# Gate and up products of 25 experts in each MoE layer as 512-column products on two column groups

## What is computed

```python
def hier_moe(h, rg_w, rg_b, re_w, re_b, w_gate, w_up, w_down):
    # top-1 of 4 groups, then top-2 of its 8 experts: 32 experts, 512 (token, expert) pairs
    ...
    def expert_block(args):
        xr, e = args
        return (jax.nn.silu(xr @ w_gate[e]) * (xr @ w_up[e])) @ w_down[e]
    ...
    out = jnp.zeros((T, D), jnp.float32).at[row_tok].add(y * row_w[:, None])
```

## Time and profile before

| | us |
|---|---|
| median of 3 runs (2040.75 to 2042.89) | 2042.81 |
| the profiled execution's own time | 2039.13 |
| its span, first to last instruction | 2037.3 |
| PE busy in the span | 1929.5 (95%) |
| DVE busy | 879.4 (43%) |
| ACT busy | 672.0 (33%) |
| first MoE layer, from its gather to its last combine | about 46 to 492 |
| second MoE layer | about 598 to 1036 |

### The profile page before, as it was taken

How to read it: one execution, slowest core, us unless ns; L and a number is a source line. 1 busy time by engine, 2 the same in 40 slices (tenths; PEclk the granted TensorE clock), 3 DMA queues, 4 the chain that set the end, 5 groups by cost and what they waited for, 6 DMA issues and landing times. The chain is left out here.

```text
span 2037.3 us, 36364 instructions
## 1 busy us (share of the span) xinstructions
PE 1929.5 (95%) x16096; PEld 1379.6 (68%) x16096; DVE 879.4 (43%) x1396; ACT 672.0 (33%) x1138; POOL 61.3 (3%) x99
## 2 busy tenths in 40 slices
PE   7999989888999999999989999999999999999998
PEld 6544444445984444434468888878888888987887
DVE  4111111104740111111165656875655665786663
ACT  2000000004530000000054546674545564675552
POOL 0000000000000000000020000010000000011000
PEclk8999999999999999999999999999999999999999
DMA  9999999998679999999975545335545555425551
GB/s 406 431 430 431 430 431 430 432 428 348 266 294 434 428 429 431 432 431 429 425 287 200 189 163 206 124 134 216 188 165 207 199 189 183 166 99 186 191 194 65
DMA packets 48992, 598.33 MB, mean 294 GB/s; under 512 B 5428, under 2 KB 5940, under 8 KB 8884
## 3 DMA queue, kind: packets, MB, share of 16 engines
q1 hardware_dynamic: 47664, 592.43, 71.9%
q10 hardware_dynamic: 1156, 3.42, 0.5%
HBM read 594.78 MB, written 1.05 MB: 292 GB/s over the span
## 5 line engine op out<-in xcount | busy, mean ns | idle before, releaser
L2006 DVE TENSOR_TENSOR SPLIT<-RING,SPLIT 128x2048 fp32r<-128x2048 f32 (+2 forms) x178 | 398.9, 2256 | 139.4 <-ACT SPLIT L1484 139.3
L1484 ACT ACTIVATE SPLIT<-RING 128x2048 fp32r<-128x2048 f32 (+2 forms) x178 | 332.7, 1887 | 42.0 <-DMA RING<-in_units 42.0
L1149 PE MATMUL PS<-HTB,SPLIT 128*128 128x512 f32 x1152 | 289.1, 393 | 0.0
L747 PE MATMUL PS<-RING,WK 128*32 128x128 f32 x8192 | 259.7, 274 | 18.0 <-issue 13.7
L781 PE MATMUL PS<-WK 128*32 128x512 f32 x560 | 250.6, 601 | 23.2 <-DVE WK L2275 20.6
L747 PEld LDWEIGHTS PS<-RING,WK 128*32 128x32 f32 x8192 | 229.7, 109 | 51.3 <-issue 48.6
L1632 ACT ACTIVATE WK<-PS 128x128 f32<-128x128 f32 x64 | 17.8, 278 | 688.0 <-PE PS L747 688.0
L1149 PEld LDWEIGHTS PS<-HTB,SPLIT 128*128 128x128 f32 x1152 | 207.4, 189 | 37.3
L781 PEld LDWEIGHTS PS<-WK 128*32 128x32 f32 x560 | 59.3, 111 | 189.3 <-issue 162.1
L2268 DVE TENSOR_TENSOR WK<-WK,PS 128x128 f32<-128x128 f32 x64 | 18.4, 288 | 341.7 <-ACT WK L1632 341.7
L1152 PEld LDWEIGHTS PS<-HTB,SPLIT 128*128 128x128 f32 x1152 | 157.2, 190 | 11.3
(11 more groups left out here) (342 smaller groups left out, 2295.1 us busy)
## 6 DMA issues: line engine op xcount, KB each, us to landing
RING<-in_w_gu SPq DMA_DIRECT2D x54, 4096.0 KB, 33.3
RING<-in_units SPq DMA_DIRECT2D x171, 1024.0 KB, 4.8
WK<-in_w_down SPq DMA_DIRECT2D x37, 2048.0 KB, 31.3
RING<-in_w_gu SPq DMA_DIRECT2D x20, 2048.0 KB, 13.6
RING<-in_w_down SPq DMA_DIRECT2D x18, 2048.0 KB, 32.1
SEAT<-in_w_down SPq DMA_DIRECT2D x7, 2048.0 KB, 34.6
RING<-in_units SPq DMA_DIRECT2D x4, 768.0 KB, 12.0
RB<-in_rows ACTq DMA_DIRECT2D x6, 512.0 KB, 3.8
```

Of the source, the lines that this page charges most:

```text
L747: t = pe.matmul(PS[32 * q:32 * q + 32, pb, z * 128:z * 128 + 128], mo.XE[:, g % 2, c, 32 * i:32 * i + 32], v[:, c, 128 * q:128 * q + 128], ...
L1149: pe.matmul(out.rearrange("p (z b n) -> p z b n", z=2, b=2), hi(c), HTB[:, :, :, c, :], start=c == 0, stop=False)
L1484: ac.activation(unit_part(u, 0), loaded(u), ACT.Copy).then_inc(s_hi, 1)
L2006: dv.tensor_tensor(unit_part(u, 1), loaded(u), unit_part(u, 0).bitcast(F32), ALU.subtract).then_inc(s_lo, 1)
```

## The change

`slim(e)` holds for experts 5 to 29 of both layers. For these:

- `gate_up` runs 16 products of 512 columns: chunk c of gate on column group 0 (outputs on partitions 0 to 31), chunk c of up on column group 1 (partitions 32 to 63), in turns. Both semaphores are raised on the last pair.
- silu reads 32 x 512 from partitions 0 to 31 of the bank and writes partitions 32 to 63 of HW (the same memory as HG); the product with up is 32 x 512 and goes to partitions 64 to 95 or 96 to 127 of HW, by the expert's parity.
- `turn_hidden` is four transposes of 32 x 128 into 128 x 32 each, one per quarter of the hidden width.
- silu waits, besides what it waited for, until the product of the expert before has been made (s_hg); where the layout changes (experts 5 and 30) until the expert before has been turned (s_ht).

The down products, the gather, the combine, the loads, and experts 0 to 4, 30 and 31 are as they were. The diff, cut to its core:

```diff
+def slim(e):
+    return 5 <= e < 30
...
             def gate_up(e):
...
+                if slim(e):
+                    pe.wait_ge(*landed(("both", l, e)))
+                    v = slab(("both", l, e))[:, 0:2 * SLOT].rearrange("p (z c n) -> p z c n", z=2, c=8)
+                    for c in range(8):
+                        if i == 0 and c % 4 == 0:
+                            pe.wait_ge(s_xe, evicted(l, g, c // 4))
+                        for z in range(2):
+                            t = pe.matmul(PS[32 * z:32 * z + 32, pb, :], mo.XE[:, g % 2, c, 32 * i:32 * i + 32],
+                                          v[:, z, c, :], start=c == 0, stop=c == 7)
+                            if c == 7:
+                                t.then_inc(s_up if z else s_gate, 1)
+                    return
...
-                pe.transpose(PS[:, 3, 0:128], mo.HG[:, 2 + e % 2, :], ident).then_inc(s_ht, 1)
+                if slim(e):
+                    rows = slice(64 + 32 * (e % 2), 96 + 32 * (e % 2))
+                    for f in range(4):
+                        t = pe.transpose(PS[:, 3, 32 * f:32 * f + 32], mo.HW[rows, 128 * f:128 * f + 128], ident[rows, rows])
+                    t.then_inc(s_ht, 1)
...
-                        ac.activation(mo.HG[:, pb, :], PS[:, pb, 0:128], ACT.Silu).then_inc(s_silu, 1)
+                        if slim(e):
+                            ac.wait_ge(*((s_hg, 32 * l + e) if slim(e - 1) else (s_ht, 32 * l + e)))
+                            ac.activation(mo.HW[32:64, :], PS[0:32, pb, :], ACT.Silu).then_inc(s_silu, 1)
+                        else:
+                            if slim(e - 1):
+                                ac.wait_ge(s_ht, 32 * l + e)
+                            ac.activation(mo.HG[:, pb, :], PS[:, pb, 0:128], ACT.Silu).then_inc(s_silu, 1)
...
-                        dv.tensor_tensor(mo.HG[:, 2 + pb, :], mo.HG[:, pb, :], PS[:, pb, 128:256],
-                                         ALU.mult).then_inc(s_hg, 1)
+                        if slim(e):
+                            dv.tensor_tensor(mo.HW[64 + 32 * pb:96 + 32 * pb, :], mo.HW[32:64, :], PS[32:64, pb, :],
+                                             ALU.mult).then_inc(s_hg, 1)
```

More of the change, by code:

```diff
@@ L342, in build @@
         mo.GT = al(512).rearrange("p (k n) -> p k n", k=2)
-        mo.HG = al(512).rearrange("p (k n) -> p k n", k=4)
+        mo.HW = al(512)
+        mo.HG = mo.HW.rearrange("p (k n) -> p k n", k=4)
         mo.HE = al(256).rearrange("p (k n) -> p k n", k=2)
@@ L763, in turn_hidden @@
                     pe.wait_ge(s_he, 32 * l + e)
-                pe.transpose(PS[:, 3, 0:128], mo.HG[:, 2 + e % 2, :], ident).then_inc(s_ht, 1)
+                if slim(e):
[4 more added lines that the diff above has]
+                else:
+                    pe.transpose(PS[:, 3, 0:128], mo.HG[:, 2 + e % 2, :], ident).then_inc(s_ht, 1)
             def down(e):
@@ L2267, in step @@
                         dv.wait_ge(s_silu, 32 * l + e + 1)
-                        dv.tensor_tensor(mo.HG[:, 2 + pb, :], mo.HG[:, pb, :], PS[:, pb, 128:256],
-                                         ALU.mult).then_inc(s_hg, 1)
+                        if slim(e):
+                            dv.tensor_tensor(mo.HW[64 + 32 * pb:96 + 32 * pb, :], mo.HW[32:64, :], PS[32:64, pb, :],
+                                             ALU.mult).then_inc(s_hg, 1)
+                        else:
+                            dv.tensor_tensor(mo.HG[:, 2 + pb, :], mo.HG[:, pb, :], PS[:, pb, 128:256],
+                                             ALU.mult).then_inc(s_hg, 1)
                     if e:
```

## The result

The change made the kernel slower, by about the amount forecast. The medians are 2192.06 us (2190.41 to 2193.38, 4 runs) after it and 2042.18 us (2040.75 to 2042.89, 4 runs) before it, a ratio of 1.0735 with a 95% interval of 1.0723 to 1.0748. The forecast was 2196, in a range of 2180 to 2225. The profiled executions stand at 2193.38 and 2039.13 us, 154.3 apart; the sum was made against that one and came to +153.

The account below looks back on a forecast made before the run. Transfers (58.9 us per group) and PE (54.6) stood close, with PE the bound after. 92.0 us per layer, 184 for both, less 22.8 and 8, gave +153: 2042.8 to 2196 us, range 2180 to 2225.

Parts of the forecast that it names:

- The bound: MoE layers: transfers at 58.9 us per group of four stand close above PE's 54.6; changed, PE bounds at 69.3.
- cover: MoE layers: PE has 4.3 us per group, about 1.1 us per expert, before a longer step makes it the bound.
- Part 1: Gate_up products: two column groups run side by side, 7.0 us instead of 3.63, +3.37 us per expert.
- Rival 4: Gate_up: the column groups take turns at 512 columns, +343 us, about 2540; 4%.
- Part 2: Steps with i = 1: gate_up starts before down ends, gaining 1.67 us each, 11.7 us per layer.
- Part 3: From gate_up's end to down: longer silu and product add 0.72 us, 0.80 for i = 0; 19.4 us per layer.
- Part 4: MoE layers: weight waits (8.2 us) and "issue" stalls (14.6) vanish, together 22.8 us, plus 8 us from half clock.
- Rival 3: The 12 spots with i = 0, between gate_up and down: clock falls anew, +20 up to 40 us, 2216 to 2236; 10%.
- Rival 2: PE's "issue" stalls in gate_up stay, so 14.6 us and 8 us of half clock come back, 2219; 9%.
- rival 5: MoE layers: not slower, the transfers stay the bound and cover it all, 2020 us; 3%.

Follow-up runs that it names:

- e4_one_in_four: Kernel before with the change for only one expert in four (5, 9, ... 29; seven a layer): 2076.93 us, ratio 1.018.
- e5_gate_then_up: Changed kernel with all eight gate products on column group 0 first, then all eight of up on group 1: 2430.43 us, single run.
- e3_clear_of_down: Changed kernel with gate and up of i = 3 (six experts a layer) on column groups 2 and 3 instead of 0 and 1: 2174.67 us.
- e1_copy_first: Changed kernel with DVE's copy of the turned hidden values put ahead of the product with up in each step: 2150.13 us, ratio 1.0527.
- e6_light_loads: Kernel before, gate and up loads for experts 8 to 29 cut to 6144 of 8192 columns (output not the reference's): 2024.51 us.
- e10_light_copy_first: Kernel before with gate and up loads of experts 8 to 29 cut to 6144 of 8192 columns, and DVE's copy ahead of the product: 2011.37 us.

## Why the prediction was right

**The bound** (PE takes over from the transfers). Right: no wait for weights is left, and a group takes 69.2 us, 69.3 forecast. What the prediction says of cover, that up to 4.3 us per group would be free, was wrong (e4_one_in_four), but its sum subtracts PE's waits and makes no use of it.

**Part 1, gate_up.** Right: 6.99 us for a forecast of 7.0. Down of experts 30 and 31 had been the proper row for whether column groups run side by side at more than 128 columns. Rival 4 falls by this number, and e5_gate_then_up shows the condition it stands on: the products for the two groups in turns.

**Part 2, the start ahead of down.** Right: from the start of down to the turn 12.17 us (170.46 to 182.63), 12.18 by the sum, and the experiments of either sign. The Trainium skill, page "TensorE: Matmul & The Clock Gate", section "The mechanism", has matmuls in strict program order; for products on different column groups no trace here agrees, from 157.44 against 158.72 to 273.71 against 274.13 in e3_clear_of_down.

**Part 3, the tail.** The mechanism was right (e1_copy_first), two sizes were off and nearly cancelled. All engines in the i = 1 step, which answers to the earlier trace rows:

```profile
182.63 0.43 PE L785 MATMUL PS<-CS,WK 32*128 32x32 f32 x4
182.77 0.59 ACT L1658 ACTIVATE WK<-PS 32x512 f32<-32x512 f32 x1 [4.62 <-PE PS L746]
183.39 0.68 DVE L2299 TENSOR_TENSOR WK<-WK,PS 32x512 f32<-32x512 f32 x1 [4.10 <-ACT WK L1658]
184.11 0.29 DVE L2309 COPY WK<-PS 128x128 f32<-128x128 f32 x1
```

silu took 0.59 and the product 0.68, as the rows of 128 partitions had it. But the copy used to start 0.09 us before the product ended, and now it starts just behind it, so the tail grew by 0.79 to 0.86 us instead of 0.72: +4 us in all. Against that, I took 0.17 us between two small turns from the turns of gate rows; four of them together take 0.43, and for i = 0 the step from the gate rows' turn to down grew from 1.83 to 2.18 us, 0.35 instead of 0.80: -5 us in all. At expert 30 it is +0.41 (1.40 for 0.99) instead of +0.7, and at expert 5 +1.17 instead of +0.96.

**Part 4, what goes away.** Right in full for the 22.8 us of waits and stalls. Of the 17.1 us of half clock in the layers 3.4 are left, in one stretch at the first changed expert of the first layer:

```profile
113.59 1.52 PE L805 MATMUL PS<-RING,WK 128*32 128x512 f32 x2 [1.80 <-DVE WK L2309]
114.10:117.40 3.30, 3.30 (x5) 0.66 (x4) 0.00 (x0) 0.00 (x0) 0.00 (x0) 0.50 0.97 417
```

There silu waits for the turn, PE stands idle for 1.80 us, and the clock fell to 1.2 GHz just behind it. The same place in the second layer has the same idle time and no fall:

```profile
739.98 7.05 PE L805 MATMUL PS<-WK 128*32 128x512 f32 x16 [1.80 <-DVE WK L2309]
740.00:743.40 3.40, 3.40 (x8) 0.88 (x9) 0.00 (x0) 0.00 (x0) 0.00 (x0) 1.00 0.99 424
```

So that idle time does not always bring a fall. A second new stretch lies outside the layers, ahead of the second one's first gather, in a stage that the change does not touch:

```profile
667.10:670.30 3.20, 3.20 (x11) 2.66 (x11) 2.26 (x18) 0.67 (x4) 0.00 (x0) 0.50 1.04 443
```

The traces of e6_light_loads and e10_light_copy_first, with PE's program of the kernel before, have one at the same place (581.9 and 578.8 us), so it is not the change that brings it. Rival 3 had looked for falls in the 12 steps with i = 0; there none happened, where PE stood idle for 0.96 and 0.38 us around the turns. The stretch that is left costs 1.7 us. The prediction gave back 8 us for all of the 17.1, and half of the 13.7 that went are 6.8.

With the measured sizes: per layer 18 x 3.36 + 7 x 1.69 for the products and 18 x 0.83 + 1.17 + 6 x 0.35 + 0.41 for the tails, 90.9 us; both 181.8; less 22.8 and 6.8 is +152.2. The layers themselves, from the first turn of gate rows to the start of the last combine (435.9 before, 508.3 after) and, in the second, to the end of it (430.5 and 509.0), grew by 151.0. The other 3.3 of the 154.3 us lie outside them, 2.1 ahead of the first layer, where half clock took 20.5 us instead of 13.7, and 1.0 between the layers, where the fall at 667 us stands. The sum had counted nothing there. Against the 151.0 us of the layers it is 2 too high, with errors that partly cancel (184 for 181.8, and 8 for 6.8), and that it comes within 1.3 of the whole is luck.

**Rival 2** falls with the 0.0 us of stalls behind the same branch, and **rival 5** with the group of 69.2 us.

## What to carry to other kernels

Where a product uses 32 of the array's 128 columns, what counts in these traces is the number of column groups that work at the same time and not the number of instructions: 16 products on two groups cost 7.0 us where 64 on four cost 3.6. When two limits stand close together, price a longer step by the waits that the trace really shows on the engine, and not by the difference of the two rates, since a lead at the start of a stage makes most of that difference worthless as cover. Nor does a full DMA settle it: 47 us more of PE's work cost 35 with the transfers at 428 GB/s as before. Before lengthening an operation, look at what stands behind it in its engine's list: here putting one copy ahead of a longer product was worth 42 us in the changed kernel and nothing in the one that transfers held.

## What was not expected of the hardware

- Matmuls on a free column group start ahead of earlier ones that wait for a busy group, by three or four records of the program (1.3 to 1.7 us at 0.43 us each), shown by the traces of the kernel before, the changed one, e3_clear_of_down and e5_gate_then_up. The choice of the group alone moved the time by +25 and -17 us.
- Stalls of PE without a releaser, 1.3 to 4.2 us long in the kernel before, need many instructions per microsecond: 8.7 us of them at 383 GB/s with 64 products per expert, none at 380 and 1.0 at 406 GB/s with 16. In six traces each ended 1.2 to 1.7 us after a packet of the instruction queue had landed.
- The same idle time of PE, 1.80 us, was followed by a fall of the clock in one layer and by none in the other.
- Four transposes of 32 x 128 take 0.43 us together, hardly more than one of 128 x 128 (0.33).
- An operation on 32 partitions x 512 took as long as one on 128 x 512: 0.59 against 0.60 us on ACT, 0.68 against 0.69 on DVE.
